# Two groups of key transposes moved into the first latent unit, and one small product moved two parts later

## The chip, the cores and the metric

The kernel runs on one core of one Trainium2 chip. The metric is the device time of one launch, in microseconds (us); lower is better. A time given for the kernel is the median of several launches; the profile is one execution of its own.

## The reference, cut to what matters

One inference step of a two-layer encoder for 512 prompt frames and 32 sample frames (544 tokens, width 1024). Each layer multiplies the tokens by one wide input matrix whose columns feed three branches (latent attention, a gated linear recurrence, a chunked MLP), merges the three through gates, and runs a SwiGLU block. The lines around the change are below. `ckv_raw` has 256 columns, made by the two latent units; `S_new` is the recurrence's state, for which the keys `k` are needed with tokens in the partitions; `o_lat` is the attention's output, here that of the 32 sample frames:

```python
cq, ckv_raw, kr_raw, hq, hf, hi, hg, cu, cv, ga, gb, gc = jnp.split(x @ lw['w_in'], idx, axis=-1)
...
ckv = rms_norm(ckv_raw, lw['kv_norm_g'])
...
S_new = jnp.exp(bL)[..., None] * S0 + jnp.einsum('bshk,bshv->bhkv', k * jnp.exp(bL[:, None] - b), v)
...
y_a = jnp.einsum('bshr,rhv->bshv', o_lat, lw['w_uv']).reshape(B, S, MLA_HEADS * MLA_D_V) @ lw['w_pa']
...
m = jax.nn.sigmoid(ga) * y_a + jax.nn.sigmoid(gb) * y_b + jax.nn.sigmoid(gc) * y_c
```

## The kernel before, in words

The program writes out each engine's instructions by hand, and the engines meet through semaphores. Tokens stand in the free dimension (544 columns, as two halves of 272), channels in the partitions. Every float32 weight is split in two: ScalarE (ACT) copies the loaded block `raw` to a rounded high half `whi`, VectorE (DVE) subtracts it to get the low half `wlo`, and TensorE (PE) adds three products, xh by whi, xl by whi and xh by wlo. The work is cut into **units**, one block of 128 output columns each. A full unit has eight **parts**, one for each 128 channels of its input; a part is six matmuls (three products, two token halves), written by `wide` (L686 to L706, its matmul at L700). A unit waits for its low half (`unit_ready`) and for one of two accumulators (`tile`, names `acc0` and `acc1`). SyncE (SP) loads the blocks ahead into four slots of `raw`; a load waits for the low half of the unit that held the slot. The high half of unit n+1 can be made once unit n-1 has been used.

Small products use four other PSUM banks in turn, the `ring`. `group` takes the next bank and waits until its last user has been copied out.

Around the first place (L1185 to L1226), once in each layer: the last of eight pairs of units for the third branch (`gc7`, `pc7`) ends. Beside them DVE scales the recurrence's queries Q, keys K and decays F level by level (`decay`, three operations each, counted by the semaphore `h_decay`; the last of 21 is an operation on F). Then `keys_to_rows(c)` (L807, matmul at L814) turns the four heads' keys of token group c by four transposes against the identity; its first call waits for the 21st count. Groups 0 and 1 are turned first. Then come the two latent units `ckv0` and `ckv1`, each followed by `chunk_out` (L831), `chunk_state` (L841, needs the turned keys copied out) and `keys_to_rows(c + 2)`. ACT's order there is: copy turned keys 0 and 1 to `Kt`, make the high half of the second latent unit, copy `ckv0` out, copy the output of `chunk_out`, copy the next turned keys.

Around the second place, `merge_a_order` writes a stage of 16 units (8 of eight parts and 8 of four) as a list of 96 slots, one for each part; `MA_STEPS` names small steps that stand behind a slot. The same function sorts ACT's and DVE's steps by due time, counted in slots. `sample_values` (L1028) makes the second half of the sample heads' latents behind slot 30, ACT copies them to `olat`, and `sample_heads` (L1038, eight products of 128 by 64 weights) multiplies them by `uvr`. Its result goes over `att` to the operands `yah` and `yal` of the first four-part unit, which begins at slot 40. Slot 32 is the first part of a unit.

Of the kernel before, what the change touches and what calls it, by code (L numbers as in the profile page):

```python
# [38 lines left out]
KD = D // P  # L39
# [18 lines left out]
U_CV, U_CU, U_HI, U_HF, U_HQ, U_HG, U_MC, U_CKV, U_CQ, U_KR = 0, 4, 8, 12, 16, 20, 24, 40, 42, 44  # L58
# [108 lines left out]
def unit_ma(n):  # L167
# [1 line left out]


MA_STEPS = {"keys0": 0, "keys1": 2, "rope_keys": 5, "scores0": 9, "probs0": 18, "scores1": 19, "values0": 21, "heads0": 23, "probs1": 28,
            "values1": 30, "heads1": 32}
MA_DUE = {"keys_out": 0.6, "new_keys": 0.5, "rope_out": 0.8, "scores_out": 1.0, "exp": 4.8, "max": 3.6, "norm": 6.6, "fill": 1.0, "probs_out": 0.8,
          "values_out": 1.5, "heads_out": 1.2, "ya_hi0": 13.0, "ya_lo0": 15.0, "ya_hi1": 2.0, "ya_lo1": 2.6,
          "tanh": 0.3, "lo": 1.5, "merge": 0.3, "m_hi": 2.4, "m_lo": 3.6}
# [89 lines left out]
def program(nc, A, OUT, ctx):  # L265
# [389 lines left out]
    def _(pe):  # L655
# [15 lines left out]
        def tile(name, layer, i=0, per=0):  # L671
            t = ntile[0]
            ntile[0] += 1
            tile_at[name] = t
            pe.wait_ge(*at(f"tile_free{t % 2}", layer, t // 2 + (per // 2) * i))
            return acc[t % 2]

        def unit_ready(layer, n, i=0, per=0):
            pe.wait_ge(*at("w_lo", layer, n + 1 + per * i))
# [46 lines left out]
        def proj(layer, n, name):  # L726

            unit_ready(layer, n)
            dst = tile(name, layer)
            wide(dst, n, KD, xh, xl).then_inc(*inc("w_used"))  # L730
# [76 lines left out]
        def keys_to_rows(layer, c):  # L807

            if c == 0:
                pe.wait_ge(*at("h_decay", layer, 21))  # L810
            g = group(f"kt{c}", layer)
            t0 = c * P if c < 4 else T - P
            for h in range(HH):
                last = pe.transpose(g[:, h * P:(h + 1) * P], K[:, h, t0:t0 + P], ident)  # L814
            last.then_inc(*inc("group_ready"))

        def chunk_out(layer, c):

            g = group(f"o{c}", layer)
            w, q0 = (P, c * P) if c < 4 else (NS, NP)  # L820
            if c == 0:
                for k in range(4):
                    pe.wait_ge(*group_freed(f"tree7_{k}", layer))
            if c == 4:
                pe.wait_ge(*at("s_load", layer, 16))
            elif c > 0:
                pe.wait_ge(*group_freed(f"st{c - 1}", layer))
            for h in range(HH):
                a = AT[:, c, h, :] if c < 4 else ATs[P - NS:P, h, :]
                v = vhi[:, c, h * P:(h + 1) * P] if c < 4 else vhi[P - NS:P, c, h * P:(h + 1) * P]  # L830
                last = pe.matmul(g[:, h * w:(h + 1) * w], v, a, start=True, stop=c == 0)  # L831
                if c > 0:
                    state = S[:, (c - 1) % 2, h, :] if c < 4 else S[:, 0, h, :]
                    last = pe.matmul(g[:, h * w:(h + 1) * w], state, Q[:, h, q0:q0 + w], start=False, stop=True)  # L834
            last.then_inc(*inc("group_ready"))

        def chunk_state(layer, c):
            g = group(f"st{c}", layer)
            pe.wait_ge(*group_freed(f"kt{c}", layer))
            for h in range(HH):  # L840
                last = pe.matmul(g[:, h * P:(h + 1) * P], Kt[:, c % 2, h * P:(h + 1) * P], vhi[:, c, h * P:(h + 1) * P],  # L841
                                 start=True, stop=True)
            last.then_inc(*inc("group_ready"))
# [330 lines left out]
        for l in layers():  # L1174
# [18 lines left out]
            for c in range(8):  # L1193
# [5 lines left out]
                    pe.wait_ge(*at("yc_lo", l, 1))  # L1199
                dst = tile(f"pc{c}", l)  # L1200
                wide(dst, n, 4, ych, ycl).then_inc(*inc("w_used"))
            keys_to_rows(l, 0)
            keys_to_rows(l, 1)
            for c in range(2):
                proj(l, U_CKV + c, f"ckv{c}")
                chunk_out(l, c)
                chunk_state(l, c)
                keys_to_rows(l, c + 2)
            def with_steps(n, count, k0, dst, start, stop, steps):
                for k in range(count):  # L1210
                    last = wide(dst, n, 1, xh, xl, k0=k0 + k, off=k * P, start=start and k == 0, stop=stop and k == count - 1)
                    if k == count - 1:
                        last.then_inc(*inc("w_used"))
                    for step, *arg in steps.get(k0 + k, ()):
                        step(l, *arg)

            unit_ready(l, U_CQ)
            dst = tile("cq0", l)
            with_steps(U_CQ, KD, 0, dst, True, True, {2 + c: [(latent_sums, 0, c)] for c in range(5)})
# [3 lines left out]
            dst = tile("cq1", l)  # L1223
# [7 lines left out]
            for n in range(2):  # L1231
                unit_ready(l, U_KR + n)
                if n == 0:
                    dst = tile("kr", l)
# [23 lines left out]
            for step, *arg in merge_b_order("PE"):  # L1258
# [5 lines left out]
                elif step == "part":  # L1264
                    n, k = arg
                    if k == 0:
                        unit_ready(l, n)
                        pair, c, part = unit_mb(n)
                        dst = tile(f"{'pb' if part else 'gb'}{c}", l)
# [18 lines left out]
            for step, *arg in merge_a_order("PE"):  # L1288
                if step == "part":
                    n, k = arg  # L1290
                    if k == 0:
                        unit_ready(l, n)
                        c, part = unit_ma(n)
                        dst = tile(f"{'pa' if part else 'ga'}{c}", l)
# [28 lines left out]
            for k in range(KD):  # L1323
                unit_ready(l, U_WO + k)
                dst = tile(f"wo{k}", l)
# [8 lines left out]
            for j in range(4):  # L1334
                unit_ready(l, U_UP + j)
                dst = tile(f"up{j}", l)
# [19 lines left out]
            with pe.Fori(1, KF // 2) as i:  # L1356
                for j in range(4):
                    unit_ready(l, U_UP + j, i, 4)
                    dst = tile(f"up{j}", l, i, 4)
# [4 lines left out]
            for c in range(8):  # L1364
                for j, (k0, kn) in enumerate(DOWN):
                    n = U_DN + 3 * c + j
                    unit_ready(l, n)
                    if j == 0:
                        dst = tile(f"dn{c}", l)
# [1403 lines left out]
```

## Time and profile before

| | |
|---|---|
| median of 3 runs | 2104.75 us (2103.08, 2104.75, 2108.36) |
| profiled execution, own time | 2103.65 us |
| its span, first to last instruction | 2101.9 us |
| mean granted TensorE clock | 0.996 of full |
| PE busy | 2073.1 us, 99% |
| DVE, ACT, POOL busy | 1158.7, 707.7, 85.4 us |
| DMA | 163.45 MB, mean 78 GB/s |

The profiled execution's own time has 1.75 us around its span and lies 1.10 us under the median. "PE" is the matmul side of TensorE. In a timeline row such as "285.69 0.41 PE ... x2", the first number is the start of the first of the two instructions, the second the time to the end of the last one; matmuls overlap, so the pace is read from start to start.

### The profile page before, as it was taken

How to read it: one execution, taken by the hardware profiler on the slowest of the kernel's cores; microseconds unless marked ns; L12 is line 12 of the kernel's file. 1: busy time of each engine (PE TensorE's matmuls, PEld its weight loads, DVE VectorE, ACT ScalarE, POOL GpSimd, SP SyncE). 2: the span in 40 equal slices, each digit the busy share in tenths (PEclk: the TensorE clock that was granted, in tenths of full speed). 3: DMA queues.
4: the chain of work that ended last, by engine and by line, in shares of the span. 5: the costliest groups of instructions: out<-in, count | busy, mean ns of one | idle time of the engine just before them, and what ended most of it. 6: DMA issues, size and time to landing. Idle time of an engine off the chain costs nothing.

```text
span 2101.9 us, 38512 instructions
## 1 busy us (share of the span) xinstructions
PE 2073.1 (99%) x16020; PEld 1995.5 (95%) x16020; DVE 1158.7 (55%) x1872; ACT 707.7 (34%) x1146; POOL 85.4 (4%) x99
## 2 busy tenths in 40 slices
PE   7999999999999999999999999999999999999999
PEld 5899999898999999999979999989889999999998
DVE  5434646764376666644454365377724866666433
ACT  4232135444343322322243221354433532232232
POOL 1000001000010000000010000010000200000110
PEclk9999999999999999999989999999999999999999
DMA  5232212321132232223323222132213323323231
GB/s 166 78 83 57 61 54 70 88 60 51 53 108 80 82 90 87 83 83 90 89 81 82 76 57 70 40 102 59 61 36 88 89 81 90 88 82 87 84 89 55
DMA packets 287876, 163.45 MB, mean 78 GB/s; under 512 B 8984, under 2 KB 279552, under 8 KB 287744
## 3 DMA queue, kind: packets, MB, share of 16 engines
q1 hardware_dynamic: 283712, 152.07, 25.7%
q0 software_dynamic: 3552, 8.36, 1.3%
q8 instruction: 100, 1.64, 0.3%
q10 hardware_dynamic: 480, 1.13, 0.2%
q14 instruction: 32, 0.26, 0.0%
HBM read 156.86 MB, written 4.66 MB: 77 GB/s over the span
## 4 chain that ended last, share of the span: by engine, by line
PE 96%; DVE 2%; ACT 1%; issue 0%; DMA 0%; DVEq 0%; ACTq 0%
PE acc L700 51%; PE acc L686 25%; PE ring L720 4%; PE ring L804 2%; PE ring L958 2%; PE ring L977 1%; PE acc L720 1%; PE ring L966 1%; PE ring L1028 1%; PE ring L1010 1%; PE ring L1248 1%; PE ring L831 0%; PE ring L841 0%; PE ring L855 0%; PE acc L847 0%; PE ring L834 0%
## 5 line engine op out<-in xcount | busy, mean ns | idle before, releaser
L1388 ACT ACTIVATE whi<-raw 128x1024 fp32r<-128x1024 f32 (+6 forms) x340 | 311.9, 917 | 723.9 <-PE acc L700 394.2
L1932 DVE TENSOR_TENSOR wlo<-raw,whi 128x1024 fp32r<-128x1024 f32 (+6 forms) x340 | 354.9, 1046 | 294.4 <-ACT whi L1388 293.3
L700 PE MATMUL acc<-xh,whi 128*128 128x272 f32 x1440 | 323.1, 305 | 0.3
L700 PE MATMUL acc<-xh,wlo 128*128 128x272 f32 x1440 | 298.7, 288 | 0.0
L700 PE MATMUL acc<-xl,whi 128*128 128x272 f32 x1440 | 298.5, 288 | 0.0
L686 PE MATMUL acc<-xh,whi 128*128 128x274 f32 (+1 forms) x1408 | 294.4, 290 | 0.0
L686 PE MATMUL acc<-xh,wlo 128*128 128x274 f32 (+1 forms) x1408 | 292.6, 289 | 0.0
L686 PE MATMUL acc<-xl,whi 128*128 128x274 f32 (+1 forms) x1408 | 292.3, 289 | 0.0
L700 PEld LDWEIGHTS acc<-xh,whi 128*128 128x128 f32 x1440 | 227.8, 189 | 15.4 <-issue 10.8
L700 PEld LDWEIGHTS acc<-xl,whi 128*128 128x128 f32 x1440 | 227.6, 189 | 0.0
L700 PEld LDWEIGHTS acc<-xh,wlo 128*128 128x128 f32 x1440 | 226.7, 189 | 0.0
L686 PEld LDWEIGHTS acc<-xh,whi 128*128 128x128 f32 x1408 | 222.0, 189 | 0.4
L686 PEld LDWEIGHTS acc<-xl,whi 128*128 128x128 f32 x1408 | 221.5, 189 | 0.0
L686 PEld LDWEIGHTS acc<-xh,wlo 128*128 128x128 f32 x1408 | 220.9, 189 | 0.0
L700 PE MATMUL acc<-hl,whi 128*128 128x272 f32 x704 | 145.9, 288 | 0.0
L700 PE MATMUL acc<-hh,whi 128*128 128x272 f32 x704 | 145.7, 288 | 0.0
L700 PE MATMUL acc<-hh,wlo 128*128 128x272 f32 x704 | 145.1, 287 | 0.0
L2602 DVE COPY small<-acc 128x2 f32<-128x2 f32 x88 | 14.0, 159 | 189.9 <-PE acc L686 189.5
L700 PEld LDWEIGHTS acc<-hh,whi 128*128 128x128 f32 x704 | 110.5, 188 | 0.2
L700 PEld LDWEIGHTS acc<-hh,wlo 128*128 128x128 f32 x704 | 110.4, 188 | 0.0
L700 PEld LDWEIGHTS acc<-hl,whi 128*128 128x128 f32 x704 | 110.3, 188 | 0.0
L2674 POOL TENSOR_TENSOR sq<-sq 128x544 f32<-128x544 f32 x24 | 40.5, 1687 | 1020.1 <-ACT sq L1468 1020.1
(417 smaller groups left out, 3105.2 us busy)
## 6 DMA issues: line engine op xcount, KB each, us to landing
raw<-in_w_in_dram SPq DMA_DIRECT2D x104, 512.0 KB, 3.7
raw<-in_w_up_dram SPq DMA_DIRECT2D x88, 512.0 KB, 3.7
raw<-in_w_down_dram SPq DMA_DIRECT2D x32, 512.0 KB, 3.8
raw<-in_w_o_dram SPq DMA_DIRECT2D x16, 512.0 KB, 3.7
raw<-in_w_down_dram SPq DMA_DIRECT2D x16, 384.0 KB, 3.3
raw<-in_w_pc_dram SPq DMA_DIRECT2D x16, 256.0 KB, 2.8
raw<-in_w_pb_dram SPq DMA_DIRECT2D x16, 256.0 KB, 2.8
raw<-in_w_pa_dram SPq DMA_DIRECT2D x16, 256.0 KB, 2.8
```

The lines of the kernel that those rows point to most:

```text
L686: last = pe.matmul(dst[:, at_:at_ + x1 - x0], wq[:, k * P:(k + 1) * P], x[:, k, x0:x1], start=k == 0 and q == 0, stop=k == KD - 1 and q == 2)
L700: last = pe.matmul(dst[:, b * 512:b * 512 + HALF], w[:, c:c + P], x[:, k0 + a, b * HALF:(b + 1) * HALF], start=start and a == 0 and q == 0 ...
L720: last = pe.matmul(dsts[c][:, 0:512], x[:, k, t0:t0 + P], w[:, a * 512:(a + 1) * 512], start=k == 0 and q == 0, stop=k == KD - 1 and q == 2)
L804: last = pe.matmul(out, K[:, h, t0:t0 + P], q, start=True, stop=True)
L958: pe.matmul(g[:, 0:nk], qp[0:QD + 4, j, c * P:(c + 1) * P], kp[0:QD + 4, j, 0:nk], start=True, stop=True).then_inc(*inc("group_ready"))
L966: last = pe.transpose(g[:, k:k + P], prob(e, nk)[:, k:k + P], ident)
L977: last = pe.matmul(g[DV * j:DV * j + DV, 0:P], vtm[:, k, h * DV:(h + 1) * DV], prob_rows(2 * p + j, NP)[:, k * P:(k + 1) * P], start=k == ...
L1010: pe.matmul(g[:, 0:n], qlat[:, k, e * P:(e + 1) * P], ckvT[:, k, ks], start=k == 0, stop=False)
L1028: last = pe.matmul(g[:, rt * P:(rt + 1) * P], ctm[:, k, rt * P:(rt + 1) * P], pTs[:, k, :], start=k == 0, stop=k == 8)
L1388: return act.activation(dst, src, ACT.Copy)
L1932: return dve.tensor_tensor(out, a, b, op)
L2674: pool.tensor_tensor(sq[:, 0, :], sq[:, 1 + (k - 1) % 2, :], sq[:, 0, :], ALU.add).then_inc(*inc("sq_sum"))
```

## The change

The loop over the two latent units no longer calls `proj`, which writes all eight parts at once, but `with_steps`, the helper that later units already use: it writes a unit part by part and calls small steps behind named parts. The two `keys_to_rows` calls ahead of the loop go behind the third part (index 2) and the fifth part (index 4) of the first latent unit. In the table, `heads1` goes from slot 32 to 34; the due times of ACT's and DVE's steps that follow from it move by two slots and pass no other step.

```diff
-            "values1": 30, "heads1": 32}
+            "values1": 30, "heads1": 34}
...
-            keys_to_rows(l, 0)
-            keys_to_rows(l, 1)
-            for c in range(2):
-                proj(l, U_CKV + c, f"ckv{c}")
-                chunk_out(l, c)
-                chunk_state(l, c)
-                keys_to_rows(l, c + 2)
             def with_steps(n, count, k0, dst, start, stop, steps):
                 for k in range(count):
                     last = wide(dst, n, 1, xh, xl, k0=k0 + k, off=k * P, start=start and k == 0, stop=stop and k == count - 1)
                     if k == count - 1:
                         last.then_inc(*inc("w_used"))
                     for step, *arg in steps.get(k0 + k, ()):
                         step(l, *arg)
 
+            for c in range(2):
+                unit_ready(l, U_CKV + c)
+                dst = tile(f"ckv{c}", l)
+                with_steps(U_CKV + c, KD, 0, dst, True, True, {} if c else {2: [(keys_to_rows, 0)], 4: [(keys_to_rows, 1)]})
+                chunk_out(l, c)
+                chunk_state(l, c)
+                keys_to_rows(l, c + 2)
```

On PE, at the end of `pc7` (accumulator 1) and the start of `ckv0` (accumulator 0), this stood in a row before; `cst` is the identity:

```order
L700 MATMUL acc1<-ych_58,wlo1 128x272 x2
L814 MATMUL ring<-cst,K_67 128x128 x8
L700 MATMUL acc0<-xh,whi0 128x272 x2
L700 MATMUL acc0<-xl,whi0 128x272 x2
L700 MATMUL acc0<-xh,wlo0 128x272 x2
```

and this stands there now, from the same matmul on:

```order
L700 MATMUL acc1<-ych_58,wlo1 128x272 x2
L700 MATMUL acc0<-xh,whi0 128x272 x2
L700 MATMUL acc0<-xl,whi0 128x272 x2
L700 MATMUL acc0<-xh,wlo0 128x272 x2
L700 MATMUL acc0<-xh,whi0 128x272 x2
L700 MATMUL acc0<-xl,whi0 128x272 x2
L700 MATMUL acc0<-xh,wlo0 128x272 x2
L700 MATMUL acc0<-xh,whi0 128x272 x2
L700 MATMUL acc0<-xl,whi0 128x272 x2
L700 MATMUL acc0<-xh,wlo0 128x272 x2
L814 MATMUL ring<-cst,K_67 128x128 x4
```

The first four of the eight transposes stand three parts (nine such rows) into `ckv0`; the other four follow two parts after them, ahead of the last three parts.

On PE, behind the sample heads' second values (L1028), this stood in a row before:

```order
L1028 MATMUL ring<-pTs_111,ctm_101 128x128 x18
L700 MATMUL acc1<-xh,whi1 128x272 x2
L700 MATMUL acc1<-xl,whi1 128x272 x2
L700 MATMUL acc1<-xh,wlo1 128x272 x2
L700 MATMUL acc0<-xh,whi0 128x272 x2
L700 MATMUL acc0<-xl,whi0 128x272 x2
L700 MATMUL acc0<-xh,wlo0 128x272 x2
L1038 MATMUL ring<-olat_112,uvr_107 64x32 x8
```

and now the last part of the unit in accumulator 1 is followed by three parts of the next one, of which these are the last two, and then by the product:

```order
L700 MATMUL acc0<-xh,whi0 128x272 x2
L700 MATMUL acc0<-xl,whi0 128x272 x2
L700 MATMUL acc0<-xh,wlo0 128x272 x2
L700 MATMUL acc0<-xh,whi0 128x272 x2
L700 MATMUL acc0<-xl,whi0 128x272 x2
L700 MATMUL acc0<-xh,wlo0 128x272 x2
L1038 MATMUL ring<-olat_112,uvr_107 64x32 x8
```

The product moved past two parts. Both pieces stand once in each of the two layers. The rows of DVE, ACT, POOL and SP are the same as before, in the same order.

## Rows read from the trace of the kernel before

**Rows 1.** The page: span, and busy time of each engine.

```profile
span 2101.9 us, 38512 instructions
PE 2073.1 (99%) x16020; PEld 1995.5 (95%) x16020; DVE 1158.7 (55%) x1872; ACT 707.7 (34%) x1146; POOL 85.4 (4%) x99
```

**Rows 2.** Waits of PE: line, waited for, us in total, times, longest.

```profile
PE ring L736 <- DMA cst<-in_consts_dram: 8.1, 1, 8.1
PE ring L720 <- DVE xl L1932: 6.9, 2, 3.7
...
PE ring L814 <- DVE F L1932: 1.9, 2, 1.0
PE ring L1038 <- ACT olat L1388: 1.8, 2, 0.9
```

**Rows 3.** Stretches, busy by engine, then granted clock, DMA share, GB/s.

```profile
285.00:298.00 13.00, 12.04 (x99) 11.82 (x99) 4.55 (x6) 4.70 (x7) 0.00 (x0) 1.00 0.07 11
524.00:552.00 28.00, 27.09 (x238) 26.68 (x238) 4.47 (x8) 8.08 (x18) 0.00 (x0) 1.00 0.07 20
```

**Rows 4.** Timeline of PE, 285.5 to 289 us, first layer.

```profile
285.69 0.41 PE L700 MATMUL acc<-ych,wlo 128*128 128x272 f32 x2
287.06 1.09 PE L814 MATMUL ring<-cst,K 128*128 128x128 f32 x8 [0.96 <-DVE F L1932]
...
288.24 0.41 PE L700 MATMUL acc<-xl,whi 128*128 128x272 f32 x2
```

**Rows 5.** Chain that ended last, 284 to 300 us: start, us, what.

```profile
288.15 6.08 PE acc L700 x48
```

**Rows 6.** Timeline of DVE and ACT, 285 to 330 us: start, us, instruction.

```profile
286.83 0.18 DVE L1932 TENSOR_TENSOR F<-F 128x16 f32<-128x16 f32 x1
...
289.95 1.23 DVE L1932 TENSOR_TENSOR wlo<-raw,whi 128x1024 fp32r<-128x1024 f32 x1 [2.32 <-ACT whi L1388]
...
287.81 1.09 ACT L1388 ACTIVATE Kt<-ring 128x512 f32<-128x512 f32 x2 [5.31 <-PE ring L814]
288.79 1.06 ACT L1388 ACTIVATE whi<-raw 128x1024 fp32r<-128x1024 f32 x1
```

**Rows 7.** Timeline of PE, 292.5 to 297 us: four key transposes.

```profile
295.86 0.60 PE L814 MATMUL ring<-cst,K 128*128 128x128 f32 x4
...
296.55 0.41 PE L700 MATMUL acc<-xl,whi 128*128 128x272 f32 x2
```

**Rows 8.** Timeline of PE, 533.5 to 536.5 us: transposes inside a unit.

```profile
534.40 0.43 PE L700 MATMUL acc<-xh,wlo 128*128 128x272 f32 x2
534.66 1.15 PE L1019 MATMUL ring<-cst,ps 128*128 128x128 f32 x9
...
535.90 0.42 PE L700 MATMUL acc<-xl,whi 128*128 128x272 f32 x2
```

**Rows 9.** Timeline of PE around the two sample heads' products, first layer.

```profile
529.36 0.41 PE L700 MATMUL acc<-xh,wlo 128*128 128x272 f32 x2
529.70 1.12 PE L1038 MATMUL ring<-olat,uvr 128*64 128x32 f32 x16
...
542.44 0.41 PE L700 MATMUL acc<-xh,wlo 128*128 128x272 f32 x2
543.76 1.09 PE L1038 MATMUL ring<-olat,uvr 128*64 128x32 f32 x16 [0.91 <-ACT olat L1388]
```

**Rows 10.** SP's waits in total, and the page's issues (to landing).

```profile
SPq L550 <- DVE wlo L1932: 1861.8, 315, 16.4
...
raw<-in_w_in_dram SPq DMA_DIRECT2D x104, 512.0 KB, 3.7
```

**Rows 11.** Timeline of ACT, DVE and PE, 540 to 552 us.

```profile
543.24 0.38 ACT L1388 ACTIVATE olat<-ring 128x256 f32<-128x256 f32 x1
...
545.70 0.29 DVE L1932 TENSOR_TENSOR yal<-att,yah 128x128 fp32r<-128x128 f32 x1 [2.15 <-ACT yah L1388]
...
550.21 0.41 PE L700 MATMUL acc<-yah,whi 128*128 128x272 f32 x2
```

## The prediction, as it was made blind

> **What bounds the kernel now.** I read the page first: TensorE is busy 99% of a span of 2101.9 us, DVE 55%, ACT 34% [rows 1]. So only what TensorE itself executes or waits for can move the time. The list of its waits comes next, and it is short. Apart from the start of the program and up to 3.7 us at each layer's first products, the two places of this change are the longest: 1.9 us in two waits at L814 for DVE's F, and 1.8 us in two waits at L1038 for ACT's `olat` [rows 2]. Each of them stands once in each layer, 1.0 and 0.9 us a time. Both places run at the full clock of 2.4 GHz: the granted clock is 1.00 in both stretches, the gaps included [rows 3]. The timelines then give each gap from start to start, which is the price that counts.
>
> **The keys' wait.** The last pair of matmuls of `pc7` starts at 285.69, the transposes at 287.06 [rows 4]. At the pace of the unit behind it (48 matmuls in 6.08 us, so 0.25 a pair and 0.76 a part of six [rows 5]) the next instruction could have started at 285.94. So 1.12 us are lost. What ends the wait is DVE's small F operation, 286.83 plus 0.18 = 287.01 [rows 6]. In the changed order `ckv0` follows `pc7` at 285.94 and the transposes come three parts later, at 285.94 + 3 x 0.76 = 288.22. That is 1.2 us after F is done, so this wait goes entirely.
>
> **Splitting the eight transposes.** Before, all eight cost 288.24 - 287.06 - 0.25 = 0.93 us, counted to the second pair after them, less one pair [rows 4]; that includes the slower first pair on return. Four of them cost 296.55 - 295.86 - 0.25 = 0.44 us by the same count [rows 7]. Nine transposes inside an open unit cost 535.90 - 534.66 - 0.25 = 0.99, and entering them took 0.26, that is 0.01 over the pair [rows 8]. So two insertions of four cost about 2 x 0.45 = 0.90 against 0.93: a gain of 0.03. The bounds: without the 0.01 for entry, 0.88 (a gain of 0.05); if each entry costs 0.09, as that of the sample heads' product does (529.70 - 529.36 - 0.25 [rows 9]), 1.06 (a loss of 0.13). I take 0.03, because the nearest rows, transposes of the same size inside a unit, show it. Together the keys give 1.12 + 0.03 = **1.15 us** a layer, bounds 0.99 and 1.17.
>
> **What queues behind the moved keys.** ACT copies both turned groups ahead of the high half of the second latent unit. A copy started 0.75 us after its transposes did [rows 4, 6]. The second group now starts at 288.22 + 0.45 + 1.52 = 290.19, so its copy (half of the pair's 1.09, with a latency, 0.6) runs from 290.94 to about 291.5; the high half then takes 1.06 to 292.5, and the low half, 0.1 later, 1.23 to 293.8 [rows 6]. Before, it was ready at 289.95 + 1.23 = 291.18. `ckv1` begins one slow first pair (0.34) before the pair at 296.55 [rows 7], at 296.21, and 1.15 earlier now: 295.06. So the margin shrinks from 5.0 to 1.25 us and the work stays hidden. Without this cover each microsecond of lateness would cost one. `chunk_state(0)` needs group 0 copied; that is done by 289.6, over 4 us before the unit's eight parts and the insertions end (292.9). The load that waits for this low half is issued about 2.6 us later; a load lands in 3.7 us [rows 10], and it is for a unit four ahead, with one unit taking 6 us. Nothing.
>
> **The sample heads' wait.** Unstalled, the first product of this kind started 0.34 us after the last pair (529.36 to 529.70); the second would so have started at 542.44 + 0.34 = 542.78 and did at 543.76 [rows 9]. Lost: **0.98 us**. `olat` is finished at 543.24 + 0.38 = 543.62 [rows 11], and ACT's order puts it behind a high half and a tanh that wait for the unit that ends before slot 32, so it comes no earlier and no later with the change. Two parts later is 542.78 + 1.52 = 544.30, which leaves 0.68 us. The product itself is unchanged, and it enters and leaves the stream once, as before. Its result is then 1.52 - 0.98 = 0.54 us later: `yal` ends at 546.5 instead of 545.99 and is wanted at 550.21 - 0.98 = 549.2 [rows 11], 2.7 us to spare. Cost nothing; on ACT only steps that wait for the next unit boundary follow.
>
> A rule is weighed here. The rows show that entering the product costs 0.09 us. The Trainium skill says (TensorEngine Tiling (Array Packing), section Key Properties) that changing the tiling mode drains TensorE, and these weights are 64 columns wide among 128 column ones. By that rule as I read it, the entry that now comes without a wait would pay for the rest of the last matmul, 0.29 - 0.13 = 0.16 us as an estimate, and the gain would be 0.07 less a layer; the two rows already hold whatever the chip does there, so the sum keeps 0.09.
>
> **The sum.** 1.15 + 0.98 = 2.13 us a layer, 4.26 in two, since the list of waits shows each twice at the same length [rows 2]. Bounds of the sum: 2 x (0.99 + 0.98) = 3.9 and 2 x (1.17 + 0.98) = 4.3. Against the profiled execution: 2103.65 - 4.26 = 2099.4. That execution lies 1.10 under the median of the three runs, so the forecast for a median is 2104.75 - 4.26 = **2100.5 us**, 0.20% less. A measurement of this kernel tells about 0.3% (6.3 us) from no change; the three runs alone spread over 5.3 us. So the expected gain is real but lies within it.
>
> **Rivals.**
> *Only one wait goes.* The keys' wait could be the end of a longer lag of DVE, so that something else, a bank of the ring or the low half, holds PE a little later in `ckv0` or behind it. Then the heads' 2 x 0.98 = 2.0 stay: 2102.8. Against it: DVE has 2.32 us without work ahead of the low half [rows 6], and every later step there has over 1.2 us. Chance 0.08.
> *The time comes back later.* TensorE would reach a wait that something with its own clock ends, a load above all: 2104.75, no change. Against it: it waits for no DMA after the first constants, and SP's queue itself waits 1861.8 us in all for low halves, so loads are ahead throughout [rows 2, 10]; the other waits follow TensorE's own results. Chance 0.05.
> *Slower: the second latent unit comes late.* Its high half stands behind the copy of key group 1 on ACT. It turns into a wait when the low half is more than 1.25 us later than I sum, and the kernel is slower than before when it is more than 1.25 + 2.13 = 3.4 us later. Were that block of `raw` also a load late (3.7 us [rows 10]), the low half would be ready at 291.5 + 3.7 + 1.06 + 0.1 + 1.23 = 297.6, which is 2.5 us late: 5.1 lost, 4.3 won, 2105.6. Against it: in the trace ACT makes this half at 288.79 with no wait for a load. Chance 0.03.
> *The split is dear.* Each entry into an open accumulation costs more than 0.13 us; only a row far from any here would make it more than 1 us in all. It is in the bounds.
>
> **How the numbers follow.** The forecast has 0.80, the rivals 0.16, and 0.04 is left for what I do not see. The range goes from 2097.7 (the lowest run of before, 2103.08, less 4.3, less 1.1 more, the distance between the profiled execution and the median) to 2104.9, just past the case in which all comes back. Faster by over 0.3% takes a gain of 6.3 us, more than the bounds allow, and only scatter could show it: 0.09. Within 0.3%: the forecast, the first two rivals and the third at its price, 0.89. Slower by over 0.3%, a lateness well past that price: 0.02.
>
> **What would show it.** In the changed profile the waits at L814 for F and at L1038 for `olat` are gone from TensorE's list. The transposes come in two groups of four, at 2.3 and 4.3 us after `pc7`'s last pair, each followed by a pair that takes 0.34 instead of 0.25. `chunk_out` starts at about 292.9 instead of 294.07. The low half of `ckv1` ends near 293.8, and `ckv1` starts without a wait at about 295.1. The second product starts 0.34 us after the pair ahead of it. The span is 4.3 us shorter, near 2097.6. I am wrong if a new wait at L700 for `wlo` stands in `ckv1`, if the groups of four cost over 0.5 us each, or if the span shrinks by less than 3 or more than 5.5 us.

## The result, and the profile after

| | before | changed |
|---|---|---|
| median of the runs, us | 2104.75 (2103.08 to 2109.14, 11 runs) | 2109.83 (2104.47 to 2111.04, 11 runs) |
| ratio of times, 95% interval | | 1.0016, 1.0009 to 1.0024 |
| profiled execution, us | 2103.65 | 2110.53 |
| its span, us | 2101.9 | 2108.6 |
| mean granted clock in it | 0.996 | 0.989 |

The forecast was 2100.5. The kernel became slower, by 0.16% as a ratio and by 5.1 us between medians: inside the 0.3% called no change, outside the range of 2097.7 to 2104.9, and in the other direction than the forecast. (The eleven runs of before are the three shown earlier and those made beside the changed kernel. Eight of the changed kernel's times lie at 2108.9 to 2111.0 us, with a mean clock of 0.989 or 0.990, and three at 2104.5 to 2105.2, with 0.991 to 0.993: the medians therefore lie further apart than the means, 2105.2 and 2108.7, to which the ratio is near.)

The page of the changed kernel, its span and the busy time of each engine (as [rows 1]):

```profile
span 2108.6 us, 38512 instructions
## 1 busy us (share of the span) xinstructions
PE 2083.2 (99%) x16020; PEld 2005.1 (95%) x16020; DVE 1158.9 (55%) x1872; ACT 707.8 (34%) x1146; POOL 85.3 (4%) x99
```

The same 16020 matmuls are there, and TensorE is again busy for 99% of a longer span. TensorE's busy time grew by 10.1 us and the span by 6.7, so the lost time is not idle time: instructions take longer. The list of TensorE's waits says the same (what waits, for what, us in total, times, longest; as [rows 2]):

```profile
PE ring L736 <- DMA cst<-in_consts_dram: 7.8, 1, 7.8
PE ring L720 <- DVE xl L1932: 7.5, 2, 3.8
PE ring L744 <- DVE xin L2153: 4.1, 4, 1.8
PE ring L958 <- issue: 0.9, 2, 0.5
PE ring L1248 <- ACT small L1664: 0.9, 2, 0.4
PE ring L855 <- PE ring L1248: 0.6, 2, 0.3
```

Both waits that the change aimed at, L814 and L1038, are gone, and none has come in their place. Now the two places themselves, on TensorE's timeline in the first layer (start, us, instruction; as [rows 4, 7, 9]):

```profile
284.27 0.41 PE L700 MATMUL acc<-ych,wlo 128*128 128x272 f32 x2
284.51 0.42 PE L700 MATMUL acc<-xh,whi 128*128 128x272 f32 x2
...
286.80 0.60 PE L814 MATMUL ring<-cst,K 128*128 128x128 f32 x4
287.15 0.50 PE L700 MATMUL acc<-xh,whi 128*128 128x272 f32 x2
287.49 0.41 PE L700 MATMUL acc<-xl,whi 128*128 128x272 f32 x2
...
288.75 0.60 PE L814 MATMUL ring<-cst,K 128*128 128x128 f32 x4
...
291.46 1.06 PE L831 MATMUL ring<-AT,vhi 128*128 128x128 f32 x8
...
545.76 0.41 PE L700 MATMUL acc<-xh,wlo 128*128 128x272 f32 x2
546.10 1.12 PE L1038 MATMUL ring<-olat,uvr 128*64 128x32 f32 x16
```

Before, `chunk_out` stood here on the same timeline:

```profile
294.07 1.05 PE L831 MATMUL ring<-AT,vhi 128*128 128x128 f32 x8
```

From the last pair of `pc7` to `chunk_out` it was 8.38 us before (285.69 to 294.07) and is 291.46 - 284.27 = 7.19 now: 1.19 less. A group of four transposes costs 287.49 - 286.80 - 0.25 = 0.44. The heads' product starts 0.34 after the pair ahead of it, where it was 1.32 [rows 9]: 0.98 less. So the executed work is 2.17 us shorter in each layer. What is late next, on ACT and DVE (two timelines, same columns; as [rows 6]):

```profile
289.39 0.60 ACT L1388 ACTIVATE Kt<-ring 128x512 f32<-128x512 f32 x1 [1.30 <-PE ring L814]
289.89 1.05 ACT L1388 ACTIVATE whi<-raw 128x1024 fp32r<-128x1024 f32 x1
...
291.05 1.23 DVE L1932 TENSOR_TENSOR wlo<-raw,whi 128x1024 fp32r<-128x1024 f32 x1 [4.84 <-ACT whi L1388]
```

This trace runs 285.69 - 284.27 = 1.42 us ahead of the one of before at this place, so the low half's end at 292.28 stands for the forecast's 293.8 (293.70 on the old axis), and `ckv1`, which begins at 293.61, has its 1.33 us to spare.

**Where the time went.** Only the granted clock is left to look at. I took it over the whole program, and not in the places of the change alone. Behind the start of the program and the boundary of the layers, where before shows the half clock too, three stretches run at half; such a stretch is called a fall below. The stretches of before (busy time and count of PE, PEld, DVE, ACT, POOL; then granted clock, DMA share, GB/s):

```profile
337.00:347.00 10.00, 9.55 (x62) 8.30 (x61) 5.87 (x13) 3.27 (x7) 0.76 (x1) 1.00 0.21 45
1372.00:1382.00 10.00, 9.55 (x60) 8.25 (x60) 6.14 (x13) 3.31 (x8) 0.76 (x1) 1.00 0.22 50
26.00:29.00 3.00, 3.00 (x8) 2.35 (x8) 3.00 (x6) 1.79 (x3) 0.00 (x0) 0.50 0.17 50
2085.90:2100.90 15.00, 12.55 (x91) 10.38 (x89) 6.66 (x17) 5.14 (x10) 0.00 (x0) 1.00 0.42 150
```

and those of the changed kernel:

```profile
335.00:337.50 2.50, 2.50 (x17) 2.15 (x16) 1.80 (x4) 0.24 (x1) 0.00 (x0) 1.00 0.00 1
337.50:347.80 10.30, 9.86 (x35) 8.54 (x36) 4.67 (x10) 3.00 (x6) 0.76 (x1) 0.50 0.29 78
347.80:350.00 2.20, 2.20 (x11) 1.78 (x10) 0.43 (x1) 1.00 (x4) 0.00 (x0) 1.00 0.00 0
1375.20:1385.40 10.20, 9.76 (x33) 8.14 (x33) 4.55 (x9) 2.83 (x6) 0.76 (x1) 0.50 0.28 77
2092.00:2102.20 10.20, 10.20 (x41) 8.88 (x40) 2.87 (x7) 4.02 (x8) 0.00 (x0) 0.50 0.23 86
24.00:26.90 2.90, 2.90 (x7) 2.32 (x8) 2.90 (x6) 1.69 (x4) 0.00 (x0) 0.50 0.82 250
```

The row of 337.00 of before and that of 337.50 of after lie over the same piece of program (the first begins 1.3 us ahead of the piece's first product, the second 1.8 us behind it): it runs at 1.00 of 2.4 GHz before and at 0.50 (1.2 GHz) after, until 347.80, at the same busy share (95.5% and 95.7%). The records show nothing idle ahead of the fall either: 2.50 of 2.50 us in the row of 335.00. But busy isn't dense: in the timelines below, a pair of products of 32 columns takes 0.33 us from start to start, and a pair of 272 columns 0.25. The second layer and the end of the program show the same, while the half clock at the start of the program is in both kernels (26 to 29 and 24 to 26.9). (The Trainium skill, in TensorE: Matmul & The Clock Gate, section Part 1: The HAM clock gate, has the clock follow how busy TensorE has recently been. The trace agrees that it has two levels and moves between them, but the column of busy time doesn't tell here which of two equally busy stretches will fall.) The piece is the sample frames' chunk: `chunk_out` and `chunk_state` of chunk 4, small products of 32 and 128 columns and single column sums, and the latent values behind them. Its timeline before:

```profile
338.32 0.40 PE L831 MATMUL ring<-ATs,vhi 32*128 32x32 f32 x2
...
340.91 1.14 PE L841 MATMUL ring<-vhi,Kt 128*128 128x128 f32 x8
...
346.26 0.39 PE L1248 MATMUL ring<-whi,ckvh 128*128 128x512 f32 x1
```

and after:

```profile
335.73 0.40 PE L831 MATMUL ring<-ATs,vhi 32*128 32x32 f32 x2
336.06 0.41 PE L834 MATMUL ring<-Q,S 128*128 128x32 f32 x2
...
338.89 2.05 PE L841 MATMUL ring<-vhi,Kt 128*128 128x128 f32 x8
...
344.29 0.76 PE L1248 MATMUL ring<-whi,ckvh 128*128 128x512 f32 x1 [0.45 <-ACT small L1664]
...
348.05 0.39 PE L1248 MATMUL ring<-whi,ckvh 128*128 128x512 f32 x1
```

The last row of each is the tenth value product. From the start of the piece to it: 7.94 us before, 12.32 after, so this fall costs 4.38 us. In the second layer the same account gives 1381.00 - 1373.05 = 7.95 before and 1383.89 - 1372.23 = 11.66 after, with the clock still down; to the point where it is up again the cost is about 4.5. The end of the program, from the normalization's first product on, begins with these rows, before and after:

```profile
2085.91 1.17 PE L1136 MATMUL ring<-ones,sq 128*128 128x1 f32 x10
2088.57 1.17 PE L1136 MATMUL ring<-ones,sq 128*128 128x1 f32 x10
```

It took 16.0 us before (2085.9 to 2101.9) and 20.0 after (2088.6 to 2108.6): 4.0.

**The account of the span**, 2108.6 - 2101.9 = +6.7 us: keys -1.19 x 2, heads -0.98 x 2, start of the program -1.4 (its first products came 0.9 earlier and fewer ran at half clock), boundary between the layers about -0.45, falls +4.4, +4.5 and +4.0. Together +6.7. In this execution the change saved what it was to save, and the clock took three times that.

### The profile page after: what moved, and what is told of

It reads as the page before. It is cut to its first block, busy times and chain, and to the rows that moved or that the text cites. A ratio compares the mean times of both kernels' runs of the same rounds, so it can differ in the third digit from the quotient of the medians.

```text
span 2108.6 us, 38512 instructions
## 1 busy us (share of the span) xinstructions
PE 2083.2 (99%) x16020; PEld 2005.1 (95%) x16020; DVE 1158.9 (55%) x1872; ACT 707.8 (34%) x1146; POOL 85.3 (4%) x99
## 4 chain that ended last, share of the span: by engine, by line
PE 98%; DVE 1%; ACT 1%; DMA 0%; issue 0%; DVEq 0%; ACTq 0%
PE acc L700 52%; PE acc L686 25%; PE ring L720 4%; PE ring L804 2%; PE ring L958 2%; PE ring L977 1%; PE acc L720 1%; PE ring L966 1%; PE ring L1028 1%; PE ring L1248 1%; PE ring L1010 1%; PE ring L841 1%; PE ring L855 0%; PE ring L831 0%; PE acc L847 0%; PE ring L834 0%
```

## The experiments

The theories, which some expectations call by letters. A: the saving moves the sparse piece earlier, to where the clock falls in it; where the piece stands in time decides, not what was changed. B: the eight fp32 transposes, now split inside an open unit, draw the falls. C: it was the chip or the hour. After the first eight runs, D: A holds in both directions, so a piece that comes later than in before falls too. All counts of clocks below are of single executions: in 107 executions of before beside these runs the mean granted clock was 0.994 or more in 95. The count is a coarse sign: only a profile shows where the clock fell, and 0.994 or more doesn't mean that it never did. e5's profile has 0.994 with a short fall in either layer and one at the end, e11's 0.995 with one fall.

| kernel | median us (range, runs) | ratio, 95% interval | mean clock 0.994 or more |
|---|---|---|---|
| changed, first | 2109.83 (2104.47 to 2111.04, 11) | 1.0016, 1.0009 to 1.0024 | 0 of 11 |
| e1 changed, again | 2109.57 (2105.82 to 2113.80, 7) | 1.0028, 1.0016 to 1.0040 | 0 of 7 |
| e2 keys only | 2107.12 (2104.75 to 2112.91, 12) | 1.0014, 1.0004 to 1.0025 | 2 of 12 |
| e3 heads only | 2105.88 (2102.58 to 2108.23, 12) | 1.0004, 0.9995 to 1.0013 | 6 of 12 |
| e4 changed, gap kept | 2108.43 (2103.14 to 2109.82, 11) | 1.0008, 0.9998 to 1.0018 | 4 of 11 |
| e5 before, less work | 2109.12 (2103.64 to 2112.67, 10) | 1.0018, 1.0007 to 1.0030 | 3 of 10 |
| e6 changed, more work | 2105.78 (2103.43 to 2112.53, 10) | 1.0006, 0.9995 to 1.0018 | 5 of 10 |
| e7 changed, spread | 2105.29 (2103.78 to 2111.53, 12) | 1.0006, 0.9997 to 1.0015 | 3 of 12 |
| e8 before, spread | 2105.61 (2103.50 to 2108.07, 12) | 0.9998, 0.9990 to 1.0007 | 12 of 12 |
| e9 changed, spread 2 | 2100.15 (2096.35 to 2104.28, 12) | 0.9976, 0.9967 to 0.9985 | 10 of 12 |
| e10 before, spread 2 | 2105.89 (2101.30 to 2107.59, 12) | 1.0000, 0.9992 to 1.0009 | 6 of 12 |
| e11 before, more work | 2108.04 (2105.56 to 2110.73, 11) | 1.0018, 1.0009 to 1.0027 | 9 of 11 |
| e12 changed, spread 2, again | 2099.20 (2096.45 to 2105.08, 9) | 0.9977, 0.9966 to 0.9988 | 8 of 9 |

The kernel before had a median of 2104.63, 2104.51, 2104.29 and 2104.18 us in the four sets (e1 to e4, e5 to e8, e9 and e10, e11 and e12).

### e1: the changed kernel again

No edit.

> The changed kernel once more, to see how often the granted clock falls in it. Theory A (the executed work is 2.17 us a layer shorter, as the trace shows, and whether the clock falls in the sparse stretch of small products from chunk_out(4) to the value products, L831 to L1248, is settled anew in each execution by where that stretch comes to lie): times in separate heaps, near 2100 without a fall, and about 4 us more for each fall; mean granted clock 0.996 without one and 0.989 with three. Theory B (the order of the change itself draws the falls, in every execution): all times 2109 to 2111, clock 0.989. Theory C (the slower result came from the conditions of that day): all times near 2100.

Measured 2109.57, ratio 1.0028, and no execution at a clock of 0.994 or more. Its profile has the falls in both layers again. C is out: the falls belong to the kernel. A as written was missed too: none of these 7 executions, and none of the first 11, is near 2100; the lowest are 2105.82 and 2104.47.

### e2 and e3: one part alone

e2 is before with the keys' move alone (the second hunk of the change), e3 before with the heads' move alone:

```
-            "values1": 30, "heads1": 32}
+            "values1": 30, "heads1": 34}
```

> Only the keys' move; the sample heads' product stands behind slot 32 again. Both theories expect the segment from the last pair of pc7 to chunk_out at 7.19 us instead of 8.38, in each layer, and the wait for olat of 0.9 us back. Theory A: a mixture of executions, the fastest near 2102.4 (2104.75 less 2 x 1.19), others 4 us and more above. Theory B, if the split transposes draw the falls: all executions at the lower clock, about 2111 to 2112.

> Only the sample heads' product moved; the keys stand as before. The wait at L1038 is gone, the wait at L814 for F is there (1.0 us in each layer). Theory A: the fastest executions near 2102.8 (2104.75 less 2 x 0.98), with falls in some others. Theory B, if the split transposes draw the falls: all executions near 2102.8 and the clock 0.996, since the keys' part is as before.

e2: 2107.12, ratio 1.0014, with falls in the piece in both layers. e3: 2105.88, ratio 1.0004, none in either layer; its profile fell at the end of the program alone. Two stretches of e3 (columns as above):

```profile
330.00:350.00 20.00, 19.25 (x130) 17.17 (x130) 11.87 (x26) 8.09 (x19) 1.20 (x2) 1.00 0.28 80
1365.00:1390.00 25.00, 24.25 (x172) 21.83 (x171) 15.11 (x31) 11.38 (x28) 2.79 (x5) 1.00 0.28 77
```

The keys stand ahead of the piece in each layer, the heads behind it. So, by these two profiles, the falls in the piece come with the keys' part, as A and B both say: one by its 1.19 us, the other by its transposes. e2's are of 3.4 us in the first layer and 10.2 in the second, so a fall has no fixed length. The heads' part brought no measured gain by itself (0.98 x 2 expected): its four fastest executions, 2102.6 to 2103.4, are where 2102.8 was expected, and half of the twelve lost the gain again at clocks of 0.993 and less; where these fell is not shown.

### e4: the keys split, their wait kept

```
+                if c == 0:
+                    pe.wait_ge(*at("h_decay", l, 21))
```

The new place of the transposes stays; TensorE waits for F at the start of `ckv0`, as long as before (2.1 us in two waits).

> The changed kernel with one wait added: the first latent unit waits for the last count of h_decay, so TensorE stands still 1.1 us ahead of it as before, and the transposes stay split inside the unit. The executed order is that of the change, the spacing of the sparse stretches of the two layers is nearer to that of before. Fall-free time by the sum: 2104.75 less 2 x 0.98 less 2 x 0.07 = 2102.7. Theory A: falls about as often as with only the heads moved. Theory B (the split draws them): falls in every execution, about 2112.

2108.43, ratio 1.0008. Its two layers answer differently within one execution:

```profile
330.00:350.00 20.00, 19.49 (x132) 17.38 (x130) 12.07 (x25) 7.43 (x19) 2.31 (x3) 1.00 0.29 82
1373.70:1383.90 10.20, 9.75 (x34) 8.47 (x35) 4.71 (x10) 3.00 (x6) 0.76 (x1) 0.50 0.29 78
```

Split transposes without a fall in the first layer: B alone can't be right. A fall in the second, where the heads' 0.98 and a different start of the layer had moved the piece: in favour of A, and no proof. The profile also has a fall at the end of the program, so what its median of 2108.43 has over the 2102.7 expected without falls is not the piece's alone.

### e5 and e6: the position without the change, the change without the position

e5 is before with ten matmuls a layer left out ahead of the piece (the output gate's products of the low half of the input in five of its eight parts, in the gate's second unit: it leaves out a part of the output gate's sum). e6 is the changed kernel with ten matmuls a layer repeated in the same place. Either is 1.26 us a layer at 0.126 us a matmul, 2.52 in all.

```
+                            if q == 1 and a > 2:
+                                continue
```

```
+                    for r in range(5):
+                        for h in range(2):
+                            pe.matmul(dst[:, h * 512:h * 512 + HALF], whi[(U_HG + k) % 2][:, 0:P], xh[:, 0, h * HALF:(h + 1) * HALF],
+                                      start=True, stop=True)
```

> The kernel before, with its keys and sample heads where they were, and ten of the 48 matmuls of one earlier unit (the second unit of the output gate, its xl by whi products of five parts) left out in each layer: 1.26 us less work ahead of the stretch, so the output gate is computed without them. Theory D: the stretch begins about 308.1 us after the rise instead of 309.3 (second layer 308.6 instead of 309.8), so the clock falls in most executions as in the changed kernel; fall-free time 2104.6 less 2.5 = 2102.1, but the median above 2105. Theory B: no more falls than in the kernel before, median 2102.1, clock 0.995.

> The changed kernel, with ten matmuls of one earlier unit (the second of the output gate) done once more ahead of it in each layer, 1.26 us of added work that changes nothing in the result. Theory D: in the first layer the stretch begins 309.9 to 310.1 us after the rise instead of 308.6 to 308.8, and the fall there is gone although the order of the change stands; second layer about 308.5 to 309, open. Median near 2103 to 2107, no slower than the changed kernel in spite of 2.5 us more work. Theory B: falls stay in both layers, median 2109.8 + 2.5 = 2112.3.

e5 has 2.52 us less to do and is slower than before: 2109.12, ratio 1.0018. Its stretches, with the transposes of before in their old place and both waits still in its list:

```profile
330.00:339.20 9.20, 9.20 (x72) 8.77 (x71) 4.74 (x9) 1.68 (x4) 0.22 (x1) 1.00 0.29 86
339.20:342.60 3.40, 3.40 (x16) 3.07 (x15) 0.86 (x4) 1.63 (x4) 0.00 (x0) 0.50 0.00 0
1373.50:1380.30 6.80, 6.35 (x23) 5.23 (x22) 3.83 (x9) 2.24 (x4) 0.76 (x1) 0.50 0.42 116
```

The profiled execution is one of e5's fastest (2104.49 us); its median ones, at clocks near 0.991, have no profile.

e6 has 2.52 us more to do than the changed kernel and doesn't show it: 2105.78, ratio 1.0006 (0.9995 to 1.0018), where the changed kernel had 1.0016 (1.0009 to 1.0024) and 1.0028 (1.0016 to 1.0040). These intervals overlap, so that it is the faster of the two isn't sure by the times alone; but 5 of its 10 executions have a mean clock of 0.994 or more, and none of the changed kernel's 18. First layer, with the split transposes:

```profile
330.00:350.00 20.00, 19.55 (x133) 17.62 (x132) 12.08 (x24) 7.42 (x19) 2.31 (x3) 1.00 0.31 87
```

Its second layer fell for 3.4 us, at 1374.1, and the end of the program for 6.8. These two are the decisive pair. Falls without the change, no fall in the first layer with it: the position does it, and the split transposes are neither needed for a fall nor enough for one. (The Trainium skill has in the same page, section Part 4: PE-mode transpose, a rule that counts transposes differently for the clock. It would have made B likely; nothing in these two runs needs it.)

**The distances.** For each profile that has the original piece I took the time from the last rise of the clock (at the start of the program, or at the boundary of the layers) to the piece's first product:

| from the rise to the piece, us | where | clock in the piece |
|---|---|---|
| 307.11, 307.28, 307.66, 308.03 | e5 layer 2, e1 layer 2, changed layer 2, e2 layer 1 | falls |
| 308.29, 308.56, 308.61, 308.75, 308.81 | e5 layer 1, e4 layer 2, e1 layer 1, e2 layer 2, changed layer 1 | falls |
| 309.09, 309.34, 309.34, 309.55 | e3 layer 2, before layer 1, e6 layer 1, e4 layer 1 | stays |
| 309.59, 309.83, 310.00 | e11 layer 2, before layer 2, e3 layer 1 | stays |
| 310.29, 311.34 | e11 layer 1, e6 layer 2 | falls |

Nine of nine fall up to 308.81, none of seven between 309.09 and 310.00, and both fall above. The kernel before stands inside a gap less than 1.5 us wide, and 1.19 us is enough to leave it. The falls of the first nine came at 310.6 us after the rise in every case, wherever the piece had begun: the instant belongs to the rise, not to the piece. The two above fell at 314.0. Read so, one account holds for all eighteen: in the eleven that fell, the piece had run for 1.8 to 3.7 us at the instant of the fall, and the seven that stayed had run for only 0.6 to 1.5 us at 310.6 and already for 4.0 to 4.9 at 314.0. It was found after the runs, and none of them was made to test it. (The Trainium skill says, again in Part 1 of that page, that the clock's monitor runs on its own timer, which a kernel's start doesn't reset. These instants agree with it; what the timer sees of the piece no run here shows.) The distance also holds the scatter of the start of the program: the time that the first products spend at half clock differs between executions. That may be why 12 of the 107 executions of before have a mean clock under 0.994; none of them has a profile.

### e7 and e8: the sparse piece filled

`chunk_out(4)` and `chunk_state(4)` are cut by heads into `sample_chunk(0)` and `sample_chunk(1)`, and the first stands among dense matmuls of the key rotation's units (e7 on the changed order, e8 on before's):

```
+            between[4] = between[4] + [(hgrn_sums, 3)]
+            between[6] = between[6] + [(sample_chunk, 0)]
...
-            chunk_out(l, 4)
-            chunk_state(l, 4)
+            sample_chunk(l, 1)
...
-            hgrn_sums(l, 3)
```

> The changed kernel, with the sparse stretch filled: the squares' sums of group 3 (L855) go into the rope-key units, and the sample chunk's output and state products are written head by head, two heads ahead of that unit's last part and two behind it. The same products are made. Theory D (the clock falls where the sparse stretch, which begins with the sample frames' chunk_out, lies too early against the last rise of the clock: in the six profiles so far it fell in all seven stretches that began 307.3 to 308.8 us after the rise and in none of the five at 309.1 to 310.0): with no stretch that sparse left, no fall near 337 or 1373 us at any distance; the wait of 0.45 us at L1248 goes too. About 2099 to 2101, mean clock 0.994 or more, and clearly faster than the changed kernel; falls in the last 20 us can still come. Theory B (the split transposes draw the falls): falls as before, 2108 to 2110.

> The same filling of the sparse stretch in the kernel before, keys and sample heads as before. Theory D: as rarely a fall as in the kernel before; 2104.6 less about 1 us for the wait at L1248, 2103.5; so the change proper is worth 4.3 us once the stretch is filled (this run less the filled changed kernel). Theory B: 2103.5 too, but then the filled changed kernel is slower than this one.

2105.29 and 2105.61: the gain of the changed order that I expected isn't there. e7's list of waits has a new row:

```profile
PE ring L1266 <- ACT small L1682: 2.6, 2, 1.3
```

The shorter piece makes TensorE reach the value products before ACT has made `hgrn_std(3)`, which stands behind a high half in its order, and this group's bank must be free before the first of four. The edit put an idle 1.3 us a layer where it took work away (e8's list has the same row), and the profiles still fell, later in the piece: e7 at 344.0 and in the second layer at 1378.2, e8 at 344.3 in the first layer alone, and both once more at the end of the program. So the edit missed its aim. One thing speaks for the filling even so: e7's pieces began 307.8 and 308.2 us after the rise, and neither fell at 310.6, where nine of nine had; they fell at 314.0.

### e9, e10 and e12: filled, and the wait mended

```
-                    dsts = [group(f"v{c}", l) for c in range(4)]
+                    dsts = []
...
+                    if n == 0:
+                        dsts.append(group(f"v{c}", l))
...
+            hgrn_std(3)
```

The last line stands right behind `next_hi(l, U_UV)` in ACT's order, and the old one is gone.

> The filled changed kernel again, mended: in its first form TensorE stood 1.3 us at the value products (L1266), because ACT copied the square root of group 3 only behind a high half that waits for the rope-key unit, and all four banks were taken before the first product; so a sparse and idle stretch was left and the clock fell at 344 us. Now ACT takes that square root ahead of it, and each bank is taken when its product begins. Theory D: the wait at the value products is gone (2.6 us in the first form), no fall between 335 and 350 or between 1370 and 1385 us at any distance from the rise; 2104.6 less 4.3 for the change, less about 1.5, that is 2098.5 to 2101 without a fall in the tail; mean clock 0.994 to 0.996. If a fall still comes there, the sparseness of this stretch is not what decides it.

> The same mended filling in the kernel before. Theory D: no falls in the stretch; 2104.6 less about 1.5 = 2103.1, clock 0.994 to 0.996. The change proper is then worth the difference to the filled changed kernel, 4.3 us by the sum of the prediction.

> The mended, filled changed kernel once more, to make its gain firm: 2096.5 without a fall, medians 2099 to 2101, ratio to the kernel before 0.997 to 0.998. It also gives one more profile for the distance at which a fall comes: none in a stretch that begins 309.1 us or more after the rise.

e9: 2100.15, ratio 0.9976; e12, the same kernel in the next set: 2099.20, ratio 0.9977. Its ratio's interval lies clear below 1, and its clock is at 0.994 or more in 18 of 21 executions, where the changed kernel's is in none of 18. "No fall" was wrong, though: in the changed order falls have become rarer, not impossible. e9's profile falls in the first layer and not in the second:

```profile
338.90:349.10 10.20, 10.20 (x35) 8.29 (x34) 6.28 (x12) 2.74 (x5) 0.76 (x1) 0.51 0.23 63
1365.00:1390.00 25.00, 24.70 (x177) 22.22 (x176) 15.50 (x32) 10.78 (x28) 4.03 (x7) 1.00 0.27 79
```

and e12's the other way round:

```profile
330.00:350.00 20.00, 19.70 (x134) 17.57 (x134) 11.42 (x25) 8.08 (x20) 1.19 (x2) 1.00 0.28 80
1370.30:1377.20 6.90, 6.90 (x23) 5.64 (x23) 5.13 (x11) 2.32 (x5) 0.76 (x1) 0.51 0.13 25
```

In before's order the filling did the opposite, and its expectation (no falls, 2103.1) was missed: e10 has 2105.89, a ratio of 1.0000, a clock of 0.994 or more in only 6 of 12 executions (before beside it: 22 of 23), and a fall of 10.2 us in the second layer of its profile. There the filled piece began 308.7 us after the rise, where before's begins at 309.8. Nor does the distance alone tell any more: of the filled pieces of e9, e10 and e12, those at 308.8, 308.7 and 307.5 us after the rise fell, all at 310.6, and those at 307.2, 308.2 and 309.1 stayed.

Neither of e12's pieces began at 309.1 us or later, so that part of its expectation wasn't tested.

Between e10 and e9, in one set, lies the change alone in a program with the filled piece: 2105.89 - 2100.15 = 5.7 us of gain by medians. Part of that is luck of the clock, since fewer of e9's executions have a low clock than of e10's. The executions at a clock of 0.996 and more lie at 2101.3 to 2102.35 in e10 and at 2096.35 to 2099.39 in e9, the lowest of each 4.95 apart. The forecast's 4.26 is near that, with the sign it was given; the other 0.7 is not accounted for.

### e11: the other side

Before, with e6's ten repeated matmuls a layer: the piece comes 1.26 us later than in before.

> The kernel before with the same 1.26 us of repeated matmuls a layer as in the more-work run; order of the keys and heads as before. It asks whether the kernel before merely happened to sit at a good distance. Theory D: the stretch begins about 310.6 us after the rise in the first layer and 311.1 in the second, later than any that stayed free so far (310.0), near the one that fell at 311.3, so falls become common: median above 2109, mean clock 0.993 or less. Rival: only stretches that begin early are at risk, and added work is plain added work: 2104.4 plus 2.5 = 2106.9, clock 0.995.

2108.04, ratio 1.0018, with the clock at 0.994 or more in 9 of 11: D's size and D's clock are both missed. The profile has one fall in the first layer (310.29 after the rise) and none in the second (309.59). The plain sum was 2104.2 + 2.5 = 2106.7; 1.3 more was measured. So there are falls on the later side too, of 6.8 us here and 3.4 in e6, where the nine of the earlier side took 3.4 to 10.2. How sure they are, two profiles don't show; the clocks of e11 say that they cost less than those of the changed kernel.

## Why the prediction was wrong

- *The keys' wait*: right. Predicted 1.15 us a layer, measured 1.19, just over the upper bound of 1.17. Groups of four cost 0.44 each where 0.45 was taken.
- *What queues behind the keys*: right. Margin predicted 1.25 us, measured 1.33, and the wait that would have taken it is in no list. One margin was summed wrongly, without effect: from 289.6 to 292.9 it is 3.3 us and not over 4; the copy of group 0 ended 3.4 us ahead of `chunk_out`.
- *The sample heads' wait*: right. 0.98 predicted and measured; `olat` ended 0.67 us ahead of the product (0.68 predicted), and `yal` 2.7 us ahead of the row that the prediction counted to (548.37 and 551.05; 2.7 predicted).
- *The rule on draining*: the entry, now without a wait, took 0.34 from the last pair to the product, 0.09 over the pace, as in the other places. The further 0.07 a layer was not to be seen.
- *The sum*: 4.26 predicted, 4.34 measured of executed work. It is right as an account of work, and wrong as a forecast.
- **The step that failed** begins at "Both places run at the full clock of 2.4 GHz: the granted clock is 1.00 in both stretches, the gaps included [rows 3]". That reading is true, but the sum took from it that everything behind a place keeps its own length when it comes earlier: it put the cost of the clock elsewhere at nothing, without a reason. The clock was read where the change is, and nowhere behind it. 50 us behind the keys stands a piece of small products that kept its clock, in the profiles here, only where it began 309.1 to 310.0 us after the last rise. Moving it by 1.19 us cost 4.38 us in the first layer and about 4.5 in the second; the end of the program, 4.0, went the same way in the profile.
- *The rivals*: none of them named this. "The time comes back later" spoke of a wait with its own clock, and had 0.05; the time did come back later, from something with a timing of its own, but in longer instructions and not in a wait. The slower rival's mechanism, a late low half, didn't happen.
- *The range and the chances*: 2104.9 was too low at the top, below even the 2105.6 that the slower rival was priced at. The prediction's own sign of being wrong came: the span was to shrink by 3 us at least, and it grew by 6.7. The 0.89 for "within 0.3%" held, through a change of the other sign.

**Shown**: the two waits went and saved their price (the timelines); the loss lies in stretches at half clock (the stretches); before's order falls when the piece comes earlier, and the changed order keeps its clock in the first layer when it comes later (e5, e6); the change gains 5 to 6 us where the piece is filled and its wait mended (e9, e10), part of it by fewer falls. **Open**: why the chip chooses these instants; how often each of the three falls occurs, since only profiles show where one is and other runs give just a mean; what decides the fall at the end of the program, which the profiles of the changed kernel and of e3 to e8 have and the others haven't, without an experiment of its own. Removing the small products' sparseness altogether wasn't tried.

## What to carry to other kernels

Read the granted clock over the whole program and compare each run's mean clock with the kernel before: a change that shortens the work and lowers the mean clock by 0.007 has lost elsewhere. On a kernel in which TensorE is never idle, look for the pieces of small products (here products of 1 to 128 columns) and treat them as the place where an earlier or later start can cost more than the change brings; to judge a small gain, take a variant with a few matmuls more and one with a few less. If such a piece can be mixed into dense work, try that as well and measure the change on top of it; here it paid together with the change (ratio 0.9976) and not without it (1.0000).

## What was not expected of the hardware

- Less work was slower: e5, 2.52 us of work less than before, gave a ratio of 1.0018 (1.0007 to 1.0030).
- The clock fell to 0.50 with TensorE busy 2.50 of 2.50 us ahead of it, and stayed there through 9.86 busy us of 10.30.
- A fall over some 10 us costs 4.4 us here, less than the 5.1 that half of it would be; the 0.45 us wait for ACT in it, for one, did not grow, while the eight products of L841 went from 1.14 us to 2.05.
- The falls of nine pieces came at 310.6 us after the last rise of the clock, though the pieces began at 307.1 to 308.8.
- On a 512 column product the two levels read 0.43 us from start to start at half clock (344.85 to 345.27 is one of them) and 0.23 at the full one.
